# Block attention and the residual: transposed blocks that cross on chip instead of through DRAM

## The chip, the core and the metric

The kernel runs on one core of a Trainium2 chip, in one launch. The metric is the device time in microseconds of an execution; a profile of one execution lies beside it. The engines are TensorE (PE), VectorE (DVE), ScalarE (ACT), GpSimd (POOL) and SyncE (SP), which issues most of the DMA.

## The reference

A chain of four mixers over 256 tokens of width 1024, in fp32: gated linear attention, then a SwiGLU and a gate, differential attention, again a SwiGLU and a gate, a short convolution, and block attention. What is changed lies in the last one and in the residual between all of them:

```python
def moba_mixer(h, w_in, q_gain, k_gain, w_out):      # 16 heads of 64; 256 tokens are one block
    q, k, v, z = jnp.split(h @ w_in, 4, axis=-1)
    q = rms_norm_2(heads(q), q_gain) * (HEAD_DIM ** -0.5)
    k = rms_norm_2(heads(k), k_gain)
    ...
        s_own = jnp.einsum('hqd,hkd->hqk', qc, k_own)
        s_own = jnp.where(own_dist[None] >= 0, s_own - slopes * own_dist, NEG)
        p = jax.nn.softmax(scores, axis=-1)
        ... jnp.einsum('hqk,hkd->hqd', p_own, v_own)
    y = out * jax.nn.silu(z)
    return y @ w_out
# around every mixer and feed-forward part: h = h + f(rms_norm(h, g))
```

The product of probabilities and values needs the probabilities with the keys on the partitions, and each projection needs h with its columns on the partitions: both are transposes.

## The kernel before, in words

**Weights.** All weights are one stream of 512 KB units. SP fetches unit n into one of 4 buffers of `raw` (`fetch`, L438), once VectorE has split the unit that lay there. ScalarE rounds a unit to `whi` (L671), VectorE takes the rest as `wlo` (L1079), in 8 buffers each, and TensorE runs 12 matmuls of 512 columns per unit (L1801): high with high, low with high, high with low. A unit of the block attention's stage is called by its number u from the stage's start (`END[MB_IN]`); there are 40.

**Order.** Each engine runs its program in order. In the block attention the order of the rest is a list by hand, `MB_ORDER`: an entry (u, step, arg) is run by TensorE ahead of unit u; ScalarE first rounds the units below u + 7 and VectorE first splits those below u + 6 (`AHEAD` is 6). SP runs in order too: what it waits for holds up every fetch behind it.

**Probabilities.** For two heads at a time TensorE makes the scores, VectorE adds the distance term and takes the maximum (`max`, L1661 to L1669), ScalarE the exponential (`exp`, L1022) into `mp` (4 buffers). Heads 8 to 15 are turned by TensorE (`pT`). Heads 0 to 7 (`MB_DIRECT`) are turned otherwise: VectorE turns 32x32 blocks in one instruction (`blk`, L1677) into `mblk` (2 buffers, a view of `p_tok`), and then the blocks have to change partitions. GpSimd's queue writes `mblk` to DRAM (`mb_out`, L627) and reads it back, block row by block row, into `mpT` (4 buffers, `mb_in`, L634). TensorE multiplies it with the values (`av`, two heads each, L2253), once `mb_land` says that both heads have landed. GpSimd's program holds the order of these trips and of the norms' powers (`mb_powers`, L599).

**Residual.** The second half of h (`second_blocks`, six times) and the first half behind the first part of a gate (`gate_blocks`, twice) go the same way on SP's queue: VectorE turns blocks into `hblk` (L1119, L1404), SP writes two parts to DRAM (L499, L512), waits for each, reads them back into `hland` (L502, L515), and ScalarE and VectorE make the high and low parts from it (L704 and L1133; L876 and L1414).

Of the kernel before, what the change touches and what calls it, by code (L numbers as in the profile page):

```python
# [17 lines left out]
F32 = mybir.dt.float32  # L18
# [5 lines left out]
P = 128  # L24
SEQ, D = 256, 1024
TT = SEQ // P
KT = D // P
NW = 512
# [6 lines left out]
B = 32  # L35
# [33 lines left out]
UNITS = END[-1]  # L69
# [15 lines left out]
def plan(first, tiles, steps, ends_first=False):  # L85
# [91 lines left out]
        (3, "sums", 0), (8, "sums", 1), (8, "unit", 0), (8, "unit", 1), (12, "max", 0), (12, "max", 1),  # L177
        (13, "blk", 0), (13, "max", 2), (14, "blk", 1), (15, "blk", 2), (16, "sums", 2), (17, "max", 3),
        (17, "max", 4), (17, "max", 5), (17, "blk", 3), (17, "blk", 4), (18, "unit", 2), (18, "max", 6),
        (18, "max", 7), (19, "sums", 3), (20, "blk", 5), (21, "blk", 6), (22, "unit", 3), (25, "max", 8),  # L180
        (25, "blk", 7), (25, "max", 9), (27, "max", 10), (27, "max", 11), (29, "zn", 0), (29, "zn", 1),
        (29, "max", 12), (30, "max", 13), (31, "y", 0), (31, "y", 1), (31, "max", 14), (31, "max", 15),
        (31, "ylo", 0), (32, "zn", 2), (32, "zn", 3), (33, "ylo", 1), (33, "y", 2), (33, "ylo", 2), (34, "y", 3),
        (35, "ylo", 3),),
}


# [53 lines left out]
def build(nc, stream, x, p, cols_d, rows_d, consts_d, wgate_d, out):  # L241
    ctx = ExitStack()
    with ctx:
# [37 lines left out]
        s = phase()  # L281
# [115 lines left out]
        h_dram = nc.dram_tensor("h_blocks", (4, P, 2 * NW), F32, kind="Internal").ap()  # L397
        cv_dram = nc.dram_tensor("cv_blocks", (8, P, NW), F32, kind="Internal").ap()
        mb_dram = nc.dram_tensor("mb_blocks", (MB_DIRECT, P, 3 * P), F32, kind="Internal").ap()
        s_dram = nc.dram_tensor("second_blocks", (len(PAIRED), 2, P, NW), F32, kind="Internal").ap()  # L400
        g_dram = nc.dram_tensor("gate_blocks", (2, TT, P, NW), F32, kind="Internal").ap()
        ffn_dram = nc.dram_tensor("ffn_blocks", (2 * FT, P, NW), F32, kind="Internal").ap()

        block = ctx.enter_context(nc.Block())
# [7 lines left out]
        def _(sp):  # L412
# [67 lines left out]
            def half_blocks(n, tile):  # L480
# [8 lines left out]
                             .rearrange("(i p w) -> p i w", i=P // B, p=P)).then_inc(sem("h_land"), 16)  # L489
                return at + 2  # L490

            def second_blocks(r, tile):

                at = END[tile] + (7 if tile == CV_IN else 8)
                fetch(done, at)
                s = PAIRED.index(tile)
                for q in range(2):
                    sp.wait_ge(sem("g_blk"), 2 * r + q + 1)
                    sp.dma_start(s_dram[s, q], sblk[:, q, :]).then_inc(sem(f"g_out{q}"), 16)  # L499
                for q in range(2):  # L500
                    sp.wait_ge(sem(f"g_out{q}"), 16 * (r + 1))
                    sp.dma_start(sland[:, q, :, :], s_dram[s, q].rearrange("q n -> (q n)")  # L502
                                 .rearrange("(i p w) -> p i w", i=P // B, p=P)).then_inc(sem(f"g_land{q}"), 16)
                return at

            def gate_blocks(n, tile):

                at = END[tile + 2] + 8
                fetch(done, at)
                for t in range(TT):  # L510
                    sp.wait_ge(sem("g_blk"), 2 * (2 * n + 1) + t + 1)
                    sp.dma_start(g_dram[n, t], gblk[:, t, :]).then_inc(sem(f"g_out{t}"), 16)  # L512
                for t in range(TT):
                    sp.wait_ge(sem(f"g_out{t}"), 16 * (2 * n + 2))
                    sp.dma_start(gland[:, t, :, :], g_dram[n, t].rearrange("q n -> (q n)")  # L515
                                 .rearrange("(i p w) -> p i w", i=P // B, p=P)).then_inc(sem(f"g_land{t}"), 16)
                return max(done, at)

            c = Count(sem)
# [29 lines left out]
            upto(done, END[MB_IN])  # L549
            done = max(done, END[MB_IN])  # L550
            done = second_blocks(5, MB_IN)
            fetch(done, UNITS)
            for t in range(TT):
                sp.wait_ge(sem("h_new"), 28 + t + 1)
# [8 lines left out]
        @block.gpsimd  # L563
        def _(pool):
            c = Count(sem)

            def step(ins):
                ins.then_inc(sem("pool_step"), 1)
                c.wait(pool, "pool_step", c.up("pool_step"))

            def power(src, mean, dst, n, scale, eps=EPS):

                step(nc.gpsimd.tensor_scalar(mean, src, scale, eps, ALU.mult, ALU.add))
                return nc.gpsimd.tensor_tensor(dst, mean, neg_half[:, 0:n], ALU.pow)

            def row_norm(j):

                pool.wait_ge(sem("stats"), 4 * (j + 1))
                step(nc.gpsimd.tensor_tensor(ms[:, j, 0, :], stats[:, j, 0, :], stats[:, j, 1, :], ALU.add))  # L579
                power(ms[:, j, 0, :], ms[:, j, 1, :], rstd[:, j, :], TT, 1.0 / D).then_inc(sem("rstd"), 1)  # L580

            step(nc.gpsimd.memset(ident, 0.0))
            nc.gpsimd.affine_select(ident, ident, pattern=[[-1, P]], compare_op=ALU.not_equal, fill=1.0, base=0,
                                    channel_multiplier=1).then_inc(sem("ident"), 1)
            nc.gpsimd.memset(neg_half[:, :], -0.5).then_inc(sem("pool_step"), 1)
            c.wait(pool, "pool_step", c.up("pool_step"))
            row_norm(0)
            for hd in range(GLA_H):
                pool.wait_ge(sem("gla_sq"), TT * (hd + 1))
                both = slice(hd, TT * GLA_H, GLA_H)  # L590
                power(oss[:, 0, both], oss[:, 1, both], oss[:, 2, both], TT, 1.0 / GLA_HV)\
                    .then_inc(sem("gla_rstd"), 1)
            for j in (1, 2, 3):
                row_norm(j)

            def head_power(m, k, ss, dst, sig_ss, signal):

                pool.wait_ge(sem(sig_ss), TT * m + k + 1)
                nc.gpsimd.tensor_tensor(dst, ss[:, 0, k * 8:(k + 1) * 8], neg_half[:, 0:8], ALU.pow)\  # L599
                    .then_inc(sem(signal), 1)  # L600

            def df_onorm(n):

                pool.wait_ge(sem("df_oss"), n + 1)
                nc.gpsimd.tensor_tensor(dss[:, 2, 4 * n:4 * n + 4], dss[:, 1, 4 * n:4 * n + 4], neg_half[:, 0:4], ALU.pow)\
                    .then_inc(sem("df_orstd"), 1)

            for _, what, arg in df_order("pool"):
                if what == "sums":
                    for k in range(TT):  # L610
                        at = slice(k * 8, (k + 1) * 8)
                        dst = dqr[:, arg // 3, at] if arg in (0, 3) else dss[:, 2, at]
                        head_power(arg, k, dss, dst, "df_ss", "df_rstd")
                elif what == "osums":
                    df_onorm(arg)
            for j in (4, 5, 6, 7):
                row_norm(j)

            def mb_powers(t):

                for k in range(TT):
                    head_power(t, k, mss, mss[:, 1 + t % 2, k * 8:(k + 1) * 8], "mb_ss", "mb_rstd")

            def mb_out(hd):

                pool.wait_ge(sem("mb_blk"), hd + 1)
                nc.gpsimd.dma_start(mb_dram[hd], mblk[:, hd % 2, :]).then_inc(sem(f"mb_out{hd % 2}"), 16)  # L627

            def mb_in(hd):

                pool.wait_ge(sem(f"mb_out{hd % 2}"), 16 * (hd // 2 + 1))
                if hd >= 4:
                    pool.wait_ge(sem("mb_av"), hd // 2 - 1)
                nc.gpsimd.dma_start(mpT[:, hd % 4, :].rearrange("p (i w) -> p i w", i=P // B),  # L634
                                    mb_dram[hd].rearrange("q n -> (q n)").rearrange("(i p w) -> p i w", i=P // B, p=P))\
                    .then_inc(sem(f"mb_land{hd // 2 % 2}"), 16)

            mb_powers(0)
            mb_powers(1)
            mb_out(0)  # L640
            mb_out(1)
            mb_in(0)
            mb_out(2)
            mb_in(1)
            mb_powers(2)
            mb_out(3)
            mb_in(2)
            mb_out(4)
            mb_in(3)
            mb_powers(3)  # L650
            mb_out(5)
            mb_out(6)
            for hd in (4, 5, 6):
                mb_in(hd)
            mb_out(7)
            mb_in(7)


        @block.scalar
        def _(act):  # L660
# [36 lines left out]
            def second_hi(j, dst, r, base):  # L697

                split_to(base + 8)
                for q in range(2):  # L700
                    act.wait_ge(sem(f"g_land{q}"), 16 * (r + 1))
                    for k in range(2):
                        kt = 4 + 2 * q + k
                        A(dst[0][:, kt, :].rearrange("p (t i b) -> p t i b", t=TT, b=B),  # L704
# [108 lines left out]
            def ffn(n, src):  # L813
# [46 lines left out]
                for half in range(2):  # L860
# [8 lines left out]
                    if half == 0:  # L869
# [1 line left out]
                        split_to(END[t + 2] + 2 + AHEAD)  # L871
                        squares(j + 1, 0)
                        for k in range(TT):
                            act.wait_ge(sem(f"g_land{k}"), 16 * (2 * n + 2))
                            for kt in range(4):
                                last = A((Y if src is X else X)[0][:, kt, k * P:(k + 1) * P].rearrange("p (i b) -> p i b", b=B),  # L876
                                         gland[:, k, :, kt * B:(kt + 1) * B], ACT.Copy, scale=norm_gain(j + 1)(kt))
# [192 lines left out]
        def _(dve):  # L1070
# [601 lines left out]
            def mb_blocks(hd):  # L1672

                dve.wait_ge(sem("mb_exp"), TT * (hd + 1))
                if hd >= 2:
                    dve.wait_ge(sem(f"mb_out{hd % 2}"), 16 * (hd // 2))
                V.transpose(mblk[:, hd % 2, :].rearrange("p (f n b) -> p f n b", f=P // B, b=B),  # L1677
                            mp[:, hd % 4, :].rearrange("p (n b f) -> p f n b", n=3, b=B)).then_inc(sem("mb_blk"), 1)
# [63 lines left out]
        def _(pe):  # L1742
# [495 lines left out]
            def mb_av(i):  # L2238
# [1 line left out]
                if i % 4 == 0:  # L2240
                    pe.wait_ge(sem("mb_in"), TT * (3 + 3 * (i // 4)))
                if 2 * i < MB_DIRECT:
                    pe.wait_ge(sem(f"mb_land{i % 2}"), 2 * 16 * (i // 2 + 1))
                else:
                    pe.wait_ge(sem("mb_pT"), 2 * (i + 1) - MB_DIRECT)
                if i % 2 == 0:
# [136 lines left out]
```

## Time and profile before

| | |
|---|---|
| median of 3 runs | 901.46 us (901.18 to 901.63) |
| the profiled execution, its span | 900.89 us, 898.7 us |
| busy: DVE, ACT, POOL | 654.6, 506.1, 63.4 us |
| DMA: bytes, mean rate | 187.47 MB, 209 GB/s |
| DRAM trips: `mb_blocks` | 8 out and 8 back, 192 KB each, GpSimd's queue |
| DRAM trips: second and gate blocks | 12 out and 12 back, 256 KB each, SP's queue |
| TensorE's granted clock | full speed (2.4 GHz) in all slices |

Times of a row are microseconds from the span's start unless it says ns. A row of a timeline merges like instructions that follow one another (x is their count), and gives in brackets how long the engine was idle before them and what ended that. The modelled ends of matmuls overlap the next ones.

### The profile page before, as it was taken

To read this page: it belongs to the slowest core of one execution; us is meant where nothing else is said; L and a number is where in the kernel's file an instruction comes from. 1 tells how busy PE (TensorE), PEld (TensorE's weight loads), DVE (VectorE), ACT (ScalarE), POOL (GpSimd) and SP (SyncE) were. 2 spreads that over 40 slices of the span, in tenths; PEclk is the share of its full clock that TensorE was granted. 3 is DMA by queue.
4 is the path that set the end of the run, shared out by engine and by line. 5 is a ranking of instruction groups with operands and counts; after the bars stand their busy time and mean duration, and the time that the engine had idled before them with its cause. 6 is when DMAs were issued, how large, how long until landed. Compare 5 with 4: busy or idle time off the path is not lost.

```text
span 898.7 us, 12238 instructions
## 1 busy us (share of the span) xinstructions
PE 892.9 (99%) x4364; PEld 737.0 (82%) x4364; DVE 654.6 (73%) x997; ACT 506.1 (56%) x820; POOL 63.4 (7%) x75
## 2 busy tenths in 40 slices
PE   9999999999999999999999999999999999999998
PEld 8988888888888888778888888888888888887777
DVE  6985478777735699997787776646679897779764
ACT  6756555444444667688564444435664544587681
POOL 0001000000000003211100000000010000215100
PEclk9999999999999999999999999999999999999999
DMA  7674458766755655424487667746568775656621
GB/s 271 197 240 143 162 189 301 277 242 243 240 194 194 227 199 201 160 97 141 139 284 265 237 239 246 254 142 231 202 220 278 260 253 192 207 200 234 227 70 47
DMA packets 76988, 187.47 MB, mean 209 GB/s; under 512 B 6852, under 2 KB 31812, under 8 KB 76936
## 3 DMA queue, kind: packets, MB, share of 16 engines
q1 hardware_dynamic: 75480, 182.99, 59.6%
q0 software_dynamic: 1024, 3.15, 1.0%
q10 hardware_dynamic: 432, 0.66, 0.2%
q8 instruction: 31, 0.51, 0.2%
q14 instruction: 21, 0.17, 0.1%
HBM read 171.83 MB, written 14.94 MB: 208 GB/s over the span
## 4 chain that ended last, share of the span: by engine, by line
PE 95%; DMA 2%; issue 2%; DVE 1%; POOL 1%; ACT 0%; DVEq 0%; POOLq 0%
PE bank L1801 84%; PE bank L1839 3%; PE bank L1854 1%; PE bank L2114 1%; PE bank L2140 1%; DMA mb_pT<-mb_blocks 1%; DMA mb_blocks<-p_tok 1%; DMA h<-x_dram 0%; PE bank L2224 0%; PE bank L2125 0%; PE bank L2253 0%; PE bank L1961 0%; PE bank L2009 0%; PE bank L2013 0%; PE bank L2100 0%
## 5 line engine op out<-in xcount | busy, mean ns | idle before, releaser
L671 ACT ACTIVATE whi<-raw 128x1024 fp32r<-128x1024 f32 x295 | 306.2, 1060 | 186.3 <-DMA raw<-stream_dram 108.8
L1079 DVE TENSOR_TENSOR wlo<-raw,whi 128x1024 fp32r<-128x1024 f32 x295 | 347.5, 1213 | 55.6 <-ACT whi L671 54.8
L1801 PE MATMUL bank<-whi,x_hi 128*128 128x512 f32 x560 | 152.5, 394 | 0.0
L1801 PE MATMUL bank<-wlo,x_hi 128*128 128x512 f32 x560 | 149.9, 389 | 0.0
L1801 PE MATMUL bank<-whi,x_lo 128*128 128x512 f32 x560 | 149.8, 389 | 0.0
L1801 PEld LDWEIGHTS bank<-wlo,x_hi 128*128 128x128 f32 x560 | 105.1, 188 | 22.3
L1801 PEld LDWEIGHTS bank<-whi,x_lo 128*128 128x128 f32 x560 | 105.1, 188 | 22.0
L1801 PEld LDWEIGHTS bank<-whi,x_hi 128*128 128x128 f32 x560 | 103.4, 188 | 21.7 <-issue 1.2
L1801 PE MATMUL bank<-whi,y_hi 128*128 128x512 f32 x396 | 108.0, 394 | 0.1
L1801 PE MATMUL bank<-wlo,y_hi 128*128 128x512 f32 x396 | 106.0, 390 | 0.0
L1801 PE MATMUL bank<-whi,y_lo 128*128 128x512 f32 x396 | 106.0, 389 | 0.0
L1801 PEld LDWEIGHTS bank<-wlo,y_hi 128*128 128x128 f32 x396 | 74.3, 188 | 15.7
L1801 PEld LDWEIGHTS bank<-whi,y_lo 128*128 128x128 f32 x396 | 74.3, 188 | 15.7
L1801 PEld LDWEIGHTS bank<-whi,y_hi 128*128 128x128 f32 x396 | 72.8, 188 | 16.0 <-issue 0.8
L824 ACT ACTIVATE ffn_silu<-bank,rstd 128x256 f32<-128x256 f32 x44 | 18.4, 471 | 76.8 <-PE bank L1801 76.8
L1303 DVE SCALAR_TENSOR_TENSOR ffn_mid<-bank,rstd,ffn_silu 128x256 f32<-128x256 f32 x44 | 19.3, 479 | 54.0 <-ACT ffn_silu L824 54.0
L1801 PE MATMUL bank<-whi,mid_hi 128*128 128x512 f32 x176 | 47.0, 389 | 0.0
L1801 PE MATMUL bank<-wlo,mid_hi 128*128 128x512 f32 x176 | 47.0, 389 | 0.0
L1801 PE MATMUL bank<-whi,mid_lo 128*128 128x512 f32 x176 | 47.0, 389 | 0.0
L1109 DVE TENSOR_TENSOR h<-h,bank 128x512 f32<-128x512 f32 x22 | 14.1, 683 | 44.7 <-PE bank L1801 44.5
L579 POOL TENSOR_TENSOR ms<-stats 128x2 f32<-128x2 f32 x8 | 4.9, 611 | 577.1 <-ACT junk L718 577.1
L1801 PEld LDWEIGHTS bank<-wlo,mid_hi 128*128 128x128 f32 x176 | 33.0, 188 | 6.9
(251 smaller groups left out, 891.4 us busy)
## 6 DMA issues: line engine op xcount, KB each, us to landing
raw<-stream_dram SPq DMA_DIRECT2D x295, 512.0 KB, 4.6
ffn_blocks<-ffn_blk SPq DMA_DIRECT2D x22, 256.0 KB, 2.0
ffn_land<-ffn_blocks SPq DMA_DIRECT2D x22, 256.0 KB, 3.7
second_blocks<-h_blk SPq DMA_DIRECT2D x8, 256.0 KB, 2.0
h_land<-second_blocks SPq DMA_DIRECT2D x8, 256.0 KB, 3.1
cv_blocks<-cv_blk SPq DMA_DIRECT2D x7, 256.0 KB, 5.2
cv_land<-cv_blocks SPq DMA_DIRECT2D x7, 256.0 KB, 3.3
h_blocks<-h_blk SPq DMA_DIRECT2D x3, 512.0 KB, 6.3
```

Of the source, the lines that this page charges most:

```text
L579: step(nc.gpsimd.tensor_tensor(ms[:, j, 0, :], stats[:, j, 0, :], stats[:, j, 1, :], ALU.add))
L671: A(whi[:, u % RING, :], raw[:, u % RAW, :], ACT.Copy).then_inc(sem("w_hi"), 1)
L824: A(sg[:, (t - tin) % 2, k, :], bank[2 * (t % 2) + k][:, 0:256], ACT.Silu, scale=rstd[:, j, k:k + 1]).then_inc(sem("ffn_silu"), 1)
L1079: V.tensor_tensor(wlo[:, u % RING, :], raw[:, u % RAW, :], whi[:, u % RING, :].bitcast(F32), ALU.subtract).then_inc(sem("w_lo"), 1)
L1109: V.tensor_tensor(h[:, t, half * HALF:(half + 1) * HALF], h[:, t, half * HALF:(half + 1) * HALF], bank[2 * (tile % 2) + t][:, :], ALU.add) ...
L1303: V.scalar_tensor_tensor(mid[:, (t - tin) % 2, :, k, :], bank[2 * (t % 2) + k][:, 256:512].rearrange("p (k n) -> p k n", k=2), rstd[:, j, ...
L1801: last = T.matmul(bank[pair + t][:, :], lhs[a][:, kt, t * P:(t + 1) * P], w[:, u % RING, kk * NW:(kk + 1) * NW], start=part != 1 and k == ...
L1839: last = T.matmul(bank[pair + hd // 2][:, hd % 2 * SEQ:(hd % 2 + 1) * SEQ], w[:, u % RING, kk * NW + hd * P:kk * NW + (hd + 1) * P], lhs[a ...
L1854: last = T.transpose(bank[b][:, k * SEQ + t * P:k * SEQ + (t + 1) * P], src[:, t, kt * P:(kt + 1) * P], ident)
L2114: last = T.matmul(bank[DF_S_BANKS[hd][m]][:, q * SEQ:(q + 1) * SEQ], dT[r, 0, hd, q * P:(q + 1) * P], dT[r, 1, hd, :], start=True, stop=True)
L2140: last = T.matmul(bank[b][:, q * SEQ + (hd % 2) * P:q * SEQ + (hd % 2 + 1) * P], daT[:, hd % 4, k * SEQ + q * P:k * SEQ + (q + 1) * P], dv ...
```

## The change

Heads 4 to 7 no longer go through DRAM. SP issues four transfers for each, one for every 32 partitions of `mblk`, straight into `mpT`; they stand at u = 22, 23, 26 and 27 of a new list for SP, behind the fetch of the units below u + 10, and wait for the block and for the `av` that frees the buffer of `mpT`. GpSimd's trips for these heads go. VectorE's `blk` of heads 5, 6 and 7 move from u = 20, 21 and 25 to 18, 24 and 24; those of 6 and 7 wait until heads 4 and 5 have crossed (`mblk` has two buffers). The residual's trips of the two kinds become four direct transfers per part (`cross`), without the wait between. Heads 0 to 3, the feed-forward's and the convolution's trips and `half_blocks` stay.

```diff
-        (18, "max", 7), (19, "sums", 3), (20, "blk", 5), (21, "blk", 6), (22, "unit", 3), (25, "max", 8),
-        (25, "blk", 7), (25, "max", 9), (27, "max", 10), (27, "max", 11), (29, "zn", 0), (29, "zn", 1),
+        (18, "max", 7), (18, "blk", 5), (19, "sums", 3), (22, "unit", 3), (24, "blk", 6), (24, "blk", 7),
+        (25, "max", 8), (25, "max", 9), (27, "max", 10), (27, "max", 11), (29, "zn", 0), (29, "zn", 1),
...
+    "sp": (
+        (22, "cross", 4), (23, "cross", 5), (26, "cross", 6), (27, "cross", 7),),
...
+            def cross(dst, src, signal):
+
+                for i in range(P // B):
+                    sp.dma_start(dst[:, i, :], src[i * B:(i + 1) * B, :]).then_inc(sem(signal), 16)
...
                 for q in range(2):
                     sp.wait_ge(sem("g_blk"), 2 * r + q + 1)
-                    sp.dma_start(s_dram[s, q], sblk[:, q, :]).then_inc(sem(f"g_out{q}"), 16)
-                for q in range(2):
-                    sp.wait_ge(sem(f"g_out{q}"), 16 * (r + 1))
-                    sp.dma_start(sland[:, q, :, :], s_dram[s, q].rearrange("q n -> (q n)")
-                                 .rearrange("(i p w) -> p i w", i=P // B, p=P)).then_inc(sem(f"g_land{q}"), 16)
+                    cross(sland[:, q, :, :], sblk[:, q, :], f"g_land{q}")
...
             done = second_blocks(5, MB_IN)
+            for u, _, hd in mb_order("sp"):
+                fetch(done, min(u + 10, UNITS))
+                done = max(done, min(u + 10, UNITS))
+                sp.wait_ge(sem("mb_blk"), hd + 1)
+                sp.wait_ge(sem("mb_av"), hd // 2 - 1)
+                for i in range(P // B):
+                    sp.dma_start(mpT[:, hd % 4, i * 3 * B:(i + 1) * 3 * B], mblk[i * B:(i + 1) * B, hd % 2, :])\
+                        .then_inc(sem(f"mb_cross{hd % 2}"), 16)
             fetch(done, UNITS)
...
-            mb_out(4)
             mb_in(3)
             mb_powers(3)
-            mb_out(5)
-            mb_out(6)
-            for hd in (4, 5, 6):
-                mb_in(hd)
-            mb_out(7)
-            mb_in(7)
...
                 dve.wait_ge(sem("mb_exp"), TT * (hd + 1))
-                if hd >= 2:
+                if hd >= 6:
+                    dve.wait_ge(sem(f"mb_cross{hd % 2}"), 64)
+                elif hd >= 2:
                     dve.wait_ge(sem(f"mb_out{hd % 2}"), 16 * (hd // 2))
...
-                    pe.wait_ge(sem(f"mb_land{i % 2}"), 2 * 16 * (i // 2 + 1))
+                    if i < 2:
+                        pe.wait_ge(sem(f"mb_land{i % 2}"), 2 * 16)
+                    else:
+                        pe.wait_ge(sem("mb_cross0"), 64 * (i - 1))
+                        pe.wait_ge(sem("mb_cross1"), 64 * (i - 1))
```

The gate's trips change as the second half's; ScalarE's waits for both count 64 where they counted 16.

## Rows read from the trace of the kernel before

**Rows 1.** The page, busy us of each engine, its share and instructions

```profile
PE 892.9 (99%) x4364; PEld 737.0 (82%) x4364; DVE 654.6 (73%) x997; ACT 506.1 (56%) x820; POOL 63.4 (7%) x75
```

**Rows 2.** TensorE's longest waits over the run: us in total, times, longest

```profile
PE bank L1897 <- DVE gla_r L1149: 1.2, 1, 1.2
PE bank L2253 <- DMA mb_pT<-mb_blocks: 1.1, 2, 0.7
PE bank L2100 <- issue: 0.3, 1, 0.3
```

**Rows 3.** Timeline of TensorE, 838 to 853: start, length, what

```profile
838.63 1.07 PE L1801 MATMUL bank<-whi,x_lo 128*128 128x512 f32 x4
840.35 0.87 PE L2253 MATMUL bank<-mb_pT,mb_v 128*64 128x256 f32 x8 [0.66 <-DMA mb_pT<-mb_blocks]
...
850.78 1.08 PE L1801 MATMUL bank<-whi,x_lo 128*128 128x512 f32 x4
852.27 0.87 PE L2253 MATMUL bank<-mb_pT,mb_v 128*64 128x256 f32 x8 [0.41 <-DMA mb_pT<-mb_blocks]
```

**Rows 4.** Timeline of GpSimd, 826 to 848

```profile
826.99 3.27 POOL L599 TENSOR_TENSOR mb_ss<-mb_ss,neg_half 128x8 f32<-128x8 f32 x2 [4.02 <-DVE mb_ss L1460]
...
835.18 0.76 POOL L634 DMA_DIRECT2D mb_pT<-mb_blocks  x1 [2.26 <-DMA mb_blocks<-p_tok]
...
847.04 0.75 POOL L634 DMA_DIRECT2D mb_pT<-mb_blocks  x1 [1.89 <-DMA mb_blocks<-p_tok]
```

**Rows 5.** Landing: mb_pT; raw from 825 to 850; second_blocks out (L499); back (L502)

```profile
DMA to landing us min/median/max: 3.2/5.3/5.9
DMA to landing us min/median/max: 3.2/5.1/5.8
DMA to landing us min/median/max: 2.0/2.0/2.0
DMA to landing us min/median/max: 2.6/3.1/4.3
```

**Rows 6.** Timeline of VectorE, 828 to 848

```profile
828.56 0.87 DVE L1677 STREAM_TRANSPOSE p_tok<-mb_p 128x384 f32<-128x384 f32 x1
829.35 1.18 DVE L1079 TENSOR_TENSOR wlo<-raw,whi 128x1024 fp32r<-128x1024 f32 x1
...
842.11 0.56 DVE L1661 SCALAR_TENSOR_TENSOR mb_s<-consts,bank 128x384 f32<-128x384 f32 x1 [4.14 <-PE bank L2224]
...
843.43 0.87 DVE L1677 STREAM_TRANSPOSE p_tok<-mb_p 128x384 f32<-128x384 f32 x1
...
845.49 2.35 DVE L1079 TENSOR_TENSOR wlo<-raw,whi 128x1024 fp32r<-128x1024 f32 x2
```

**Rows 7.** Timeline of SP: fetches of raw 31, 32 and 35

```profile
832.45 0.33 SPq L438 DMA_DIRECT2D raw<-stream_dram  x1
834.79 0.33 SPq L438 DMA_DIRECT2D raw<-stream_dram  x1
846.73 0.33 SPq L438 DMA_DIRECT2D raw<-stream_dram  x1
```

**Rows 8.** Windows: length, busy of each engine, TensorE's clock, DMA share, GB/s

```profile
830.00:840.00 10.00, 9.70 (x50) 7.65 (x46) 7.12 (x8) 7.60 (x11) 3.63 (x6) 1.00 0.95 330
840.00:855.00 15.00, 14.24 (x85) 10.38 (x86) 10.56 (x22) 8.78 (x20) 1.31 (x2) 1.00 0.51 180
```

**Rows 9.** Last second_blocks, then first gate_blocks: ScalarE and TensorE; SP for the gate

```profile
769.54 0.91 ACT L704 ACTIVATE x_hi<-h_land,cols 128x256 fp32r<-128x256 f32 x2 [3.40 <-DMA h_land<-second_blocks]
773.07 1.07 PE L1801 MATMUL bank<-whi,x_hi 128*128 128x512 f32 x4
...
319.02 0.33 SPq L512 DMA_DIRECT2D gate_blocks<-h_blk  x1
325.08 1.28 ACT L876 ACTIVATE y_hi<-h_land,cols 128x128 fp32r<-128x128 f32 x4 [1.48 <-DMA h_land<-gate_blocks]
327.61 1.16 PE L1801 MATMUL bank<-whi,y_hi 128*128 128x512 f32 x4
```

More of the change, by code:

```diff
@@ L399, in build @@
         mb_dram = nc.dram_tensor("mb_blocks", (MB_DIRECT, P, 3 * P), F32, kind="Internal").ap()
-        s_dram = nc.dram_tensor("second_blocks", (len(PAIRED), 2, P, NW), F32, kind="Internal").ap()
-        g_dram = nc.dram_tensor("gate_blocks", (2, TT, P, NW), F32, kind="Internal").ap()
         ffn_dram = nc.dram_tensor("ffn_blocks", (2 * FT, P, NW), F32, kind="Internal").ap()
@@ L495, in second_blocks @@
                 fetch(done, at)
-                s = PAIRED.index(tile)
                 for q in range(2):
                     sp.wait_ge(sem("g_blk"), 2 * r + q + 1)
-                    sp.dma_start(s_dram[s, q], sblk[:, q, :]).then_inc(sem(f"g_out{q}"), 16)
-                for q in range(2):
-                    sp.wait_ge(sem(f"g_out{q}"), 16 * (r + 1))
-                    sp.dma_start(sland[:, q, :, :], s_dram[s, q].rearrange("q n -> (q n)")
-                                 .rearrange("(i p w) -> p i w", i=P // B, p=P)).then_inc(sem(f"g_land{q}"), 16)
+                    cross(sland[:, q, :, :], sblk[:, q, :], f"g_land{q}")
                 return at
@@ L511, in gate_blocks @@
                     sp.wait_ge(sem("g_blk"), 2 * (2 * n + 1) + t + 1)
[L512 to L516, printed above, removed]
+                    cross(gland[:, t, :, :], gblk[:, t, :], f"g_land{t}")
                 return max(done, at)
@@ L631, in mb_in @@
                 pool.wait_ge(sem(f"mb_out{hd % 2}"), 16 * (hd // 2 + 1))
-                if hd >= 4:
-                    pool.wait_ge(sem("mb_av"), hd // 2 - 1)
                 nc.gpsimd.dma_start(mpT[:, hd % 4, :].rearrange("p (i w) -> p i w", i=P // B),
@@ L700, in second_hi @@
                 for q in range(2):
-                    act.wait_ge(sem(f"g_land{q}"), 16 * (r + 1))
+                    act.wait_ge(sem(f"g_land{q}"), 64 * (r + 1))
                     for k in range(2):
@@ L873, in ffn @@
                         for k in range(TT):
-                            act.wait_ge(sem(f"g_land{k}"), 16 * (2 * n + 2))
+                            act.wait_ge(sem(f"g_land{k}"), 64 * (2 * n + 2))
                             for kt in range(4):
```

## The prediction

> **What bounds the kernel now.** I read the page's busy times first: TensorE is busy for 892.9 of the span's 898.7 us [rows 1]. A change to transfers adds and removes no matmul, so it can only act on the 5.8 us in which TensorE is idle. The waits of TensorE over the whole run say what these are [rows 2]: the only ones that transfers of the changed kind end are two at L2253, 1.1 us together, for mb_pT. The reader is to see that no residual trip is in that list. The timeline of TensorE places the two [rows 3]: av(2) starts at 840.35 after 0.66 us idle and av(3) at 852.27 after 0.41 us. The modelled end of the matmuls before them hides about 0.1 us of each (back to back, the next group starts 0.91 us after the last: 838.63 + 0.91 = 839.54 and 850.78 + 0.91 = 851.69, so at most 0.81 and 0.58). **The most that this change can give by these waits is therefore 1.1 to 1.4 us, 0.12 to 0.15%.** A measurement of this kernel tells about 0.2%, 1.8 us, from no change; the forecast can hardly leave that band on the fast side.
>
> Next come the views of what ends the two waits. GpSimd's timeline [rows 4]: head 5's way back from DRAM is issued at 835.18, head 7's at 847.04. 835.18 + 5.2 is the end of the first wait, 847.04 + 5.2 that of the second (the trips back land in 3.2 to 5.9, median 5.3 [rows 5]). VectorE's timeline [rows 6] says why head 7 is so late: it stands idle for 4.14 us until TensorE's scores(4), turns max(8), and only at 843.43 turns blk(7), though the list has the exponentials of head 7 at u = 20.
>
> **The change part by part** (times are those of the profiled execution: 900.89 us with a span of 898.7; the median of the runs shown is 901.46, 0.57 above it, and I add that at the end).
>
> *Heads 4 to 6 in VectorE's order.* One transpose takes a place of 0.79 us (828.56 to 829.35 [rows 6]). blk(5) now stands ahead of the split of unit 24, so this split, that of unit 25 and sums(3) are 0.79 late; after blk(5)'s old place all is on time again, and after blk(6)'s old place 0.79 early. Late splits send raw 28 and 29 0.79 late, both before 830 still, while TensorE takes unit 28 only behind av(3), after 852 [rows 3]: hidden under 20 us. GpSimd's powers, which wait for sums(3), end at 831.05 instead of 830.26 [rows 4]. VectorE's unit(3), which waits for them, stood two splits of 1.1 and blk(6) behind 829.35, at 832.34, and now at 831.55: hidden with 0.5 to spare, and late by what is over that if the cover is gone.
>
> *Cross 4 and 5 on SP.* SP has to have fetched raw 31 before cross 4 and raw 32 before cross 5. These were issued at 832.45 and 834.79, each behind a split [rows 7]; 0.79 earlier that is 831.66 and 834.00. The waits added are met by then: the blocks of heads 4 and 5 are turned at u = 17 and 18 of VectorE's list, ahead of these splits, and av(0) stands at u = 22, three units ahead of the av(2) that TensorE reaches at 839.54. (At three units of 2.72 us, three groups of 0.907, it is about 8 us earlier, 831; if it came later, cross 4 and all behind it would wait with it.) An issue takes 0.33 us on SP [rows 7], four take 1.3: cross 4 until 833.3, ahead of raw 32; cross 5 from 834.3 to 835.65; raw 33, queued behind it, can go at 835.65; its split, about 1.15 behind that of raw 32 (two take 2.35 [rows 6]), allows it at 835.15: held 0.5, less than the 0.79 that its split is early. So no weight is late by SP.
>
> *How long a direct transfer takes* is not in this trace: none goes from SBUF to SBUF. From the last issue to the landing I bound it by 2.0 us below (a 256 KB write of h_blk, always 2.0 [rows 5]) and 5.8 above (raw in this stretch, 3.2 to 5.8 [rows 5]); I exclude less than 2.0, since the transfer still has a read and a write side like that one. Value taken: 3.1, the median of the read that puts 512-byte pieces on 128 partitions [rows 5], the nearest in form. The load matters: the DMA engines are 95% busy from 830 to 840 at 330 GB/s, 51% from 840 to 855 [rows 8]. The change takes one of the two trips of each head away, 192 KB or 0.6 us at that rate, so the crowd thins a little. Head 5 thus lands at 835.65 + 3.1 = 838.75 (837.65 to 841.45). TensorE is there at 839.54: the first wait goes; at the upper end it is 1.9 instead of 0.8.
>
> *The added waits on VectorE.* blk(6) now waits for cross 4 and blk(7) for cross 5, and behind them on VectorE stand the split of unit 30 and max(8). The cover is the 4.14 us in which VectorE waited for scores(4) anyway. blk(7) and that split take 0.79 + 1.14, so max(8) can start at 838.75 + 2.0 = 840.75; scores(4) releases it at 842.11 - 0.8 = 841.3 if TensorE is earlier. So max(8) at M = 841.3, and the wait costs nothing until head 5 lands later than 839.3. With 5.8 us M is 843.45.
>
> *Cross 6 and 7.* In the old order the split of unit 31 starts at 845.49, 3.38 after max(8); with blk(7) no longer between them 2.59. Raw 35 followed the start of that split by 1.24 [rows 6, 7]: now M + 3.83 = 845.1. Then SP issues cross 6 (1.3), raw 36 at 846.8 (0.5 later than its split allows, for a unit that TensorE takes eight units behind av(3)), cross 7 at 847.1 to 848.45. Landing with 3.1: 851.55 (850.45 to, with both late, 843.45 + 7.15 + 5.8 = 856.4). TensorE, 0.81 earlier, reaches av(3) at 850.9. Of the second wait 0.65 us stays instead of 0.58.
>
> *Sum at av(3):* it starts at 851.6 instead of 852.27: 0.7 us gained; with 2.0 us transfers everything, up to 1.4; with 5.8 us ones 4.1 lost. What is late next is the same wait, at the same place, for a transfer on another queue.
>
> *The residual's trips* (six second_blocks, two gate_blocks). Each replaces four issues of 0.33 us [rows 9] and a wait for writes that land in 2.0 [rows 5] by eight issues: 2.6 us of SP against 1.3 and the part of 2.0 that the second issue doesn't cover. Raw is at most some 0.5 later by that, a fifth of a unit's 2.72. At the last of the six ScalarE waited 3.40 us for the first part, had it at 769.54 and was done at 770.45; TensorE takes it at 773.07 [rows 9], 2.6 us later. From the trip before (2.0 + 0.33 + 2.6 to 4.3, 4.9 to 6.6) to the direct one (1.3 + 2.0 to 5.8, 3.3 to 7.1) the landing moves by -3.3 to +2.2: TensorE gets nothing and loses nothing. The tightest of the eight is the first gate trip: ScalarE has its last part from 325.08, is done with it at 326.36, and TensorE takes it at 327.61 [rows 9]. Direct, issued at 319.02 to 320.3, it lands at 322.3 to 326.1, at worst 1.0 after today, inside 1.25. I cost all eight at nothing.
>
> *A rule against it.* The trace's raw loads 31 and 32 are issued 2.34 us apart, and raw lands in 3.2 to 5.8 there [rows 5, 7], so neighbours on SP's queue overlap. The Trainium skill, "DMA: Bandwidth & Descriptors", "Rules for kernel authors", says that transfers under 64 KB mostly pay overhead and that two transfers to disjoint halves of the partitions serialize, so that one is to be used; each piece here is 48 KB. If the overhead overlaps as for raw, the sum above holds; if it is paid four times in a row, rival 3 does.
>
> **Rivals.**
> 1. *The wait is only moved.* Cross 7 stands on SP behind raw 35 and 36, two 512 KB loads, where GpSimd's queue passed them. If it lands 4 us after its last issue, at 852.45, av(3) starts where it did: 901.5. For it: median 5.1 of raw here [rows 5]; against: DMA only half busy after 840 [rows 8]. Taken with all outcomes from 0.2 gained to 1.8 lost.
> 2. *Slower by one chain through VectorE.* blk(7) holds VectorE until head 5 has landed; beyond 839.3 each us delays max(8), the splits 31 and 32, raw 35 and 36, and with them cross 7, which then also lands late. It decides when a transfer takes over about 4.7 us from its last issue: head 5 at 840.35, M = 842.35, av(3) at 842.35 + 7.15 + 4.7 = 854.2, 1.9 lost. With 5.5: 841.15, 843.15, 855.8, 3.5 lost: 905.0. For it: 95% load before 840 [rows 8]; against: 3.1 for the similar read.
> 3. *The four don't overlap.* 4 x 2.0 from the first issue: head 5 at 842.3, M = 844.3, cross 7 issued from 850.1 and landed at 858.1: 5.8 lost, 907.3. Against it: the overlap of the raws.
> 4. *More than 1.8 us faster* needs TensorE idle time that its waits don't list; I see none.
>
> **How the numbers follow.** Forecast, 0.2 to 1.4 gained, 0.58; rival 1, 0.27; rival 2, 0.09; rival 3, 0.03; rival 4, 0.03. Time: 901.46 - 0.7 = 900.8 (a profile of 900.2). Range: from 901.46 - 1.4 = 900.0 to 901.46 + 1.3 = 902.8, which leaves out the last two rivals and the worse part of rival 2. Faster by over 0.2%: 0.03; slower: 0.09 + 0.03 = 0.12; the rest, 0.85, within 0.2%.
>
> **What would show it.** In the profile after: L2253's wait at av(2) gone and one of at most 0.8 us left at av(3), on a direct transfer; VectorE waiting at blk(6) or blk(7) up to about 839.5 and no longer as much at max(8); raw 35 issued near 845 instead of 846.73; direct landings of 3 to 4 us from the first of the four; ScalarE's waits at L704 some 2 us shorter each and TensorE unmoved by them. Landings over 5 us, a wait of several us at av(2) or av(3), or a TensorE wait at a residual trip would make it wrong.

## The result

| | this kernel | the kernel before |
|---|---|---|
| median of 13 runs each | 904.41 us (902.96 to 905.58) | 901.18 us (899.37 to 904.40) |
| ratio, 95% interval | 1.0037 (1.0028 to 1.0045) | |
| the profiled execution, its span | 904.99 us, 903.0 us | 900.89 us, 898.7 us |

The change made the kernel 3.2 us slower. The forecast was 900.8, and 902.8 was its upper end: it was wrong, on the side of rival 2.

The page's busy times, against [rows 1]:

```profile
PE 894.8 (99%) x4364; PEld 739.1 (82%) x4364; DVE 655.0 (73%) x997; ACT 507.6 (56%) x820; POOL 59.6 (7%) x67
```

The span grew by 4.3 us and TensorE's busy time by 1.9 with the same 4364 matmuls: some is new waiting, some the same matmuls at a lower clock. TensorE's longest waits (us in total, times, longest; L2254 is the old L2253):

```profile
PE bank L2254 <- DMA mb_pT<-p_tok: 2.2, 1, 2.2
PE bank L1894 <- DVE gla_r L1144: 1.2, 1, 1.2
PE bank L2254 <- issue: 1.1, 1, 1.1
```

Two waits stand at the place of [rows 2], and both are longer. The profile names a direct transfer for one of them only; the other, at av(2), ends at 841.29, the moment at which VectorE's blk(7) starts behind the crossing of head 5 (841.30, below). TensorE's timeline (start, length, what; idle before it in brackets), against [rows 3]:

```profile
841.29 0.87 PE L2254 MATMUL bank<-mb_pT,mb_v 128*64 128x256 f32 x8 [1.05 <-issue]
...
855.04 0.87 PE L2254 MATMUL bank<-mb_pT,mb_v 128*64 128x256 f32 x8 [2.24 <-DMA mb_pT<-p_tok]
...
861.42 1.08 PE L1798 MATMUL bank<-whi,x_hi 128*128 128x512 f32 x4
```

This execution runs 0.54 us late from before the crossings (the scores that started at 814.95 start at 815.49); that differs from execution to execution, and an execution of the change with other residual shapes (`shapes`, below) has 815.02. av(2) is 0.94 later than before, 0.40 beyond that; av(3) 2.77 later, 1.83 more; the unit that started at 857.08 is 4.34 later, another 1.57. The windows (length, busy us of PE, PEld, DVE, ACT and POOL with counts, TensorE's granted clock, DMA share, GB/s) show what the last step is:

```profile
855.00:857.00 2.00, 1.96 (x17) 1.31 (x18) 0.97 (x3) 0.89 (x2) 0.00 (x0) 0.89 0.83 322
857.00:859.00 2.00, 2.00 (x7) 1.71 (x7) 1.77 (x5) 1.27 (x2) 0.00 (x0) 0.50 0.44 180
859.00:861.00 2.00, 2.00 (x8) 1.56 (x8) 1.23 (x1) 1.97 (x4) 0.00 (x0) 0.76 0.00 0
861.00:863.00 2.00, 2.00 (x10) 1.64 (x9) 0.91 (x3) 1.90 (x5) 0.00 (x0) 1.00 0.78 250
```

The clock falls to half, 1.2 GHz, behind the idle time at av(3), for some 3.4 us in all (2.00 x (0.11 + 0.50 + 0.24), over 0.5); before, it was 1.00 here. So the 4.3 us are 0.54 + 0.40 + 1.83 + 1.57.

Why head 7 came late is read from SP's timeline, against [rows 7]:

```profile
832.66 2.51 SPq L554 DMA_DIRECT2D mb_pT<-p_tok  x4
835.22 0.59 SPq L438 DMA_DIRECT2D raw<-stream_dram  x1
835.90 3.13 SPq L554 DMA_DIRECT2D mb_pT<-p_tok  x4
...
847.07 0.33 SPq L438 DMA_DIRECT2D raw<-stream_dram  x1
847.50 2.49 SPq L554 DMA_DIRECT2D mb_pT<-p_tok  x4
850.03 0.59 SPq L438 DMA_DIRECT2D raw<-stream_dram  x1
851.04 2.49 SPq L554 DMA_DIRECT2D mb_pT<-p_tok  x4
```

Four direct issues hold SP for 2.5 to 3.1 us, not 1.3, and a fetch right behind them 0.59 instead of 0.33. The groups by line (ns of one issue, min/median/max, first and last start; then the landing in us, counted from the start of the issue): the probabilities, then the residual.

```profile
L554 SPq DMA_DIRECT2D mb_pT<-p_tok x16: 542/603/1247, 832.7 to 852.9; - x16
DMA to landing us min/median/max: 2.0/2.8/4.7
L495 SPq DMA_DIRECT2D h_land<-h_blk x48: 542/603/662, 123.0 to 769.6; - x48
DMA to landing us min/median/max: 2.1/2.1/2.6
```

On the way itself the direct transfers are not slow: 2.0 to 4.7, where the way back from DRAM alone took 3.2 to 5.9 [rows 5].

VectorE's timeline, against [rows 6], shows the delay being passed on:

```profile
839.35 0.88 DVE L1674 STREAM_TRANSPOSE p_tok<-mb_p 128x384 f32<-128x384 f32 x1 [3.59 <-DMA mb_pT<-p_tok]
841.30 0.89 DVE L1674 STREAM_TRANSPOSE p_tok<-mb_p 128x384 f32<-128x384 f32 x1 [1.07 <-DMA mb_pT<-p_tok]
...
843.21 0.55 DVE L1656 SCALAR_TENSOR_TENSOR mb_s<-consts,bank 128x384 f32<-128x384 f32 x1
...
845.83 2.35 DVE L1074 TENSOR_TENSOR wlo<-raw,whi 128x1024 fp32r<-128x1024 f32 x2
```

The first two are blk(6), waiting for head 4's crossing, and blk(7), for head 5's. max(8) and the split of unit 31 stand behind them, raw 35 waits for that split, cross 6 stands behind raw 35 and cross 7 behind raw 36. **So the late end of the first two crossings comes back, through VectorE and SP's fetches, as a late start of the last two**, which then pay the same price again.

### The profile page after: what moved, and what is told of

Its sections match the earlier page's. It is cut to its first block, busy times and chain, and to the rows that moved or that the text cites. A ratio compares the mean times of both kernels' runs of the same rounds, so it can differ in the third digit from the quotient of the medians.

```text
span 903.0 us, 12271 instructions
## 1 busy us (share of the span) xinstructions
PE 894.8 (99%) x4364; PEld 739.1 (82%) x4364; DVE 655.0 (73%) x997; ACT 507.6 (56%) x820; POOL 59.6 (7%) x67
## 3 DMA queue, kind: packets, MB, share of 16 engines
q0 software_dynamic: 512, 1.57, 0.5%
## 4 chain that ended last, share of the span: by engine, by line
PE 94%; DVE 3%; DMA 1%; issue 1%; SPq 1%; ACT 0%; ACTq 0%; DVEq 0%
PE bank L1798 82%; PE bank L1836 3%; PE bank L1851 1%; DVE wlo L1074 1%; PE bank L2111 1%; PE bank L2137 1%; SPq L554 1%; DMA mb_pT<-p_tok 1%; DMA raw<-stream_dram 1%; PE bank L2221 0%; PE bank L2122 0%; PE bank L2254 0%; PE bank L1894 0%; DVE mb_tok L1462 0%; PE bank L1958 0%
## 5 line engine op out<-in xcount | busy, mean ns | idle before, releaser
L583 POOL TENSOR_TENSOR ms<-stats 128x2 f32<-128x2 f32 x8 | 1.8, 228 | 580.0 <-ACT junk L713 580.0
```

## The experiments

Theory A: an issue on SP between two places in SBUF costs 0.60 us instead of 0.33, and the order couples the last crossings to the first. Rivals: the residual's transfers do it; direct transfers are slow on the way; the shape of a piece sets the price; any queue would do as badly. Ratios are to the kernel before on the same chip; its medians there were 901.55 (23 runs; `residual_only`, `block_only`, `uncoupled`, `shapes`), 901.46 (35 runs; `pairs`, `pairs_behind`, `on_gpsimd`, `dram_earlier`) and 900.64 (15 runs; `dram_quarters`, `pairs_sums_first`). They are not the quotients of the two medians and differ from these by up to 0.001.

**One part alone: the residual.** (`residual_only`) Block attention as before.

```diff
-                    sp.dma_start(s_dram[s, q], sblk[:, q, :]).then_inc(sem(f"g_out{q}"), 16)
-                ... (the wait and the way back)
+                    cross(sland[:, q, :, :], sblk[:, q, :], f"g_land{q}")
```

> Only the residual's trips direct; heads 4 to 7 go through DRAM on GpSimd's queue as before. Theory A: no change within 0.1% (-0.5 to +0.7 us): SP is held some 5 us per trip, but TensorE has no wait there. Rival B: +1 us or more, with a new wait of TensorE or weights late near 130, 325, 450, 650, 660 or 770 us.

901.72 us (12 runs), 0.9995 (0.9984 to 1.0006): no difference that the interval shows.

**One part alone: block attention.** (`block_only`) The changed kernel with the residual's trips through DRAM.

```diff
-                    cross(sland[:, q, :, :], sblk[:, q, :], f"g_land{q}")
+                    sp.dma_start(s_dram[s, q], sblk[:, q, :]).then_inc(sem(f"g_out{q}"), 16)
+                ... (the wait and the way back)
```

> Only the block attention's part of the change (SP list, four direct transfers for each of heads 4 to 7, the blocks turned sooner); the residual's trips go through DRAM as before. Theory A (the block attention's crossings on SP cost all of it: each of their issues holds SP about 0.6 us instead of the 0.33 that I took, so cross 7 lands some 2 us late, and TensorE's clock falls behind the long wait): as much slower than before as the whole change, +2.5 to +4 us, with a wait of about 2 us at av(3). Rival B (the residual's 48 transfers, which now hold SP 5 us per trip, make weights late somewhere): clearly less than the whole change, under +2 us.

904.63 us (5 runs), 1.0036 (1.0023 to 1.0049): the whole loss. Its timeline of TensorE has the same late av(3):

```profile
855.27 0.87 PE L2260 MATMUL bank<-mb_pT,mb_v 128*64 128x256 f32 x8 [2.19 <-DMA mb_pT<-p_tok]
```

**The coupling cut.** (`uncoupled`) The last crossings stand ahead of raw 35 and 36; price and number of the issues stay.

```diff
-        (22, "cross", 4), (23, "cross", 5), (26, "cross", 6), (27, "cross", 7),),
+        (22, "cross", 4), (23, "cross", 5), (24, "cross", 6), (24, "cross", 7),),
```

> The whole change, but cross 6 and 7 stand at u = 24 in SP's list (behind raw 33 instead of raw 35 and 36): the same transfers at the same price on SP. Theory A with its second half (the place behind raw 35 and 36, whose splits follow max(8) and max(9), is what makes head 7 late): cross 7 is issued from about 843 and lands by 848, av(3) does not wait, TensorE's clock stays at full speed, only the wait of about 1 us at av(2) is left: before -0.5 to +0.8 us. Rival C (the price on SP alone, wherever the transfers stand: SP is held 10 us in this stage and weights or VectorE are late by it): still +1.5 us or more.

901.33 us (11 runs), 0.9995 (0.9986 to 1.0004): the loss is gone. TensorE's timeline, then SP's:

```profile
841.90 0.87 PE L2254 MATMUL bank<-mb_pT,mb_v 128*64 128x256 f32 x8 [0.95 <-issue]
...
853.38 0.87 PE L2254 MATMUL bank<-mb_pT,mb_v 128*64 128x256 f32 x8
```

```profile
837.32 2.48 SPq L554 DMA_DIRECT2D mb_pT<-p_tok  x4
839.85 0.59 SPq L438 DMA_DIRECT2D raw<-stream_dram  x1
840.54 6.24 SPq L554 DMA_DIRECT2D mb_pT<-p_tok  x8
```

The eight last issues span 6.24 us, but are done at 846.8 instead of 853.5. av(3) waits for nothing; av(2) still does (it starts with VectorE's blk(7), at 841.90, behind the crossing of head 5).

**Half the issues.** (`pairs`) Two heads cross in one set of four pieces of 96 KB; for that the blocks of two heads lie interleaved in `mblk` and `mpT`.

```diff
-        (22, "cross", 4), (23, "cross", 5), (26, "cross", 6), (27, "cross", 7),),
+        (22, "cross", 4), (24, "cross", 6),),
...
-                    sp.dma_start(mpT[:, hd % 4, i * 3 * B:(i + 1) * 3 * B], mblk[i * B:(i + 1) * B, hd % 2, :])\
+                    sp.dma_start(mpT2[:, hd // 2 % 2, i * 6 * B:(i + 1) * 6 * B], mblk2[i * B:(i + 1) * B, :])\
```

> Two heads per transfer as in pairs_behind, and the second set at u = 24, behind raw 33. Theory A: neither wait is left, av(2) and av(3) start without idle time: before -0.8 to -1.6 us (about 900.3 for a before of 901.5). Rival D: a wait at av(2) stays because the larger transfers land later: before +-0.5 us.

900.28 us (12 runs), 0.9986 (0.9977 to 0.9994). Its list of TensorE's longest waits has no transfer; an issue of twice the bytes costs the same:

```profile
PE bank L1897 <- DVE gla_r L1147: 1.2, 1, 1.2
PE bank L2210 <- DVE mb_tok L1465: 0.5, 1, 0.5
```

```profile
L557 SPq DMA_DIRECT2D mb_pT<-p_tok x8: 549/603/631, 833.5 to 843.1; - x8
```

**Half the issues, coupling kept.** (`pairs_behind`) As pairs, with the last crossing behind the fetches again.

```diff
-        (22, "cross", 4), (24, "cross", 6),),
+        (22, "cross", 4), (27, "cross", 6),),
```

> The change with two heads per transfer: the blocks of heads 4 and 5 (6 and 7) lie side by side, so four transfers of 96 KB carry both; they stand at u = 22 and at u = 27, behind raw 36 as the change's cross 7. SP's time for heads 4 to 7 is halved (8 issues in place of 16), the place of the last behind raw 35 and 36 is kept. Theory A (the price of an issue on SP, times sixteen, in the chain through VectorE and SP): head 5 lands about 838, max(8) is at about 842, the last transfers are issued from 847.5 to 850 and land at about 852: a wait of at most 0.8 us at av(3), clock at full speed, before -0.8 to +0.5 us. Rival D (the place behind raw 35 and 36 alone costs it, whatever the price; or a transfer twice as large holds SP twice as long): still +1.5 us or more.

902.15 us (12 runs), 1.0009 (0.9998 to 1.0020). Its interval lies under the changed kernel's (1.0028 to 1.0045), but reaches from the kernel before to rival D's 1.5 us, so the wait decides. av(3) waits half as long as in the changed kernel, though longer than theory A's 0.8:

```profile
852.96 0.87 PE L2256 MATMUL bank<-mb_pT,mb_v 128*64 128x256 f32 x8 [1.07 <-DMA mb_pT<-p_tok]
```

So the two causes act together, and each can be taken away by itself: cutting the coupling removes the wait at av(3) and leaves the one at av(2); halving the issues removes the one at av(2) and halves the one at av(3); only both together (`pairs`) leave none.

**Another queue.** (`on_gpsimd`) The same 16 transfers, issued by GpSimd behind its powers.

```diff
+            for hd in range(4, MB_DIRECT):
+                pool.wait_ge(sem("mb_blk"), hd + 1)
+                pool.wait_ge(sem("mb_av"), hd // 2 - 1)
+                ... nc.gpsimd.dma_start for the four pieces; SP's list is empty
```

> The change with the same 16 direct transfers issued by GpSimd instead of SP, each behind the same waits; SP only fetches. Theory A (SP's time is what they cost): both waits gone or under 0.3 us, before -0.5 to -1.6 us. Rival E (a direct transfer is slow by itself, on any queue, or GpSimd issues four as slowly: 0.55 to 0.75 us each): a wait of 0.5 us or more at av(2) stays: before -0.5 to +0.5 us or worse.

904.57 us (12 runs), 1.0025 (1.0014 to 1.0036): slow again, against theory A, at the other wait. GpSimd's timeline, then TensorE's:

```profile
828.44 6.03 POOL L595 TENSOR_TENSOR mb_ss<-mb_ss,neg_half 128x8 f32<-128x8 f32 x2 [4.77 <-DVE mb_ss L1453]
834.43 4.39 POOL L648 DMA_DIRECT2D mb_pT<-p_tok  x8
```

```profile
843.52 1.55 PE L2252 MATMUL bank<-mb_pT,mb_v 128*64 128x256 f32 x8 [3.12 <-DMA mb_pT<-p_tok]
```

An issue costs 0.55 us here (4.39 over 8). On this queue that is no price of the kind: in the kernel before, its writes of 192 KB to DRAM cost as much.

```profile
L627 POOL DMA_DIRECT2D mb_blocks<-p_tok x8: 540/554/758, 806.3 to 844.6; - x8
```

The powers ahead of the issues took 6.03 us instead of 3.27 [rows 4], which I had not reckoned with, so the first issue comes 1.8 us later than SP's (834.43 against 832.66). Even so the eight are out by 838.82, no later than SP's (839.03). What is late is the landing of head 5: av(2) starts 4.7 us after the last issue is done, against 2.3 in the changed kernel. Here the time on the way makes most of the wait; why it is longer is open. The run therefore doesn't say what SP's time alone is worth.

**What shape costs.** (`shapes`) One execution, 904.69 us: the residual's pieces in other shapes (the output is then another permutation of the blocks).

```diff
+                    elif form == "straight":
+                        sp.dma_start(dst[:, i, :], src[:, i * P:(i + 1) * P]).then_inc(sem(signal), 16)
+                    ... (32 partitions to the same 32; 64 partitions to 128)
```

> The whole change, but the residual's direct transfers have other shapes (the first second half: 128 partitions of 512 bytes to the same partitions; the first gate as in the change, 32 partitions of 2 KB to 128 of 512 bytes; the second second half: 32 partitions of 2 KB to the same 32; the second gate: 64 partitions of 1 KB to 128 of 512 bytes; the last two second halves as in the change), so the data that these put into h's transposed form is another permutation and the output is not the reference's. If the price of 0.54 to 0.66 us per issue comes from one source row being cut over four partitions, the straight and the quarter form take about 0.33 and the half form something between; if it comes from a transfer within SBUF as such, all take 0.54 to 0.66.

In turn: 128 partitions to the same 128, 32 to the same 32, 64 to 128, and 32 to 128 as in the change:

```profile
L498 SPq DMA_DIRECT2D h_land<-h_blk x8: 560/601/610, 122.4 to 126.9; - x8
L500 SPq DMA_DIRECT2D h_land<-h_blk x8: 590/591/607, 447.1 to 451.5; - x8
L503 SPq DMA_DIRECT2D h_land<-h_blk x8: 523/603/617, 641.8 to 646.6; - x8
L496 SPq DMA_DIRECT2D h_land<-h_blk x24: 553/603/1410, 317.2 to 769.3; - x24
```

None of the four shapes sets the price.

**The same pieces with DRAM at one end.** (`dram_quarters`) The kernel before, whose residual goes out and back in four pieces of 64 KB each.

```diff
-                    sp.dma_start(s_dram[s, q], sblk[:, q, :]).then_inc(sem(f"g_out{q}"), 16)
+                    for i in range(P // B):
+                        sp.dma_start(s_dram[s, q][i * B:(i + 1) * B, :], sblk[i * B:(i + 1) * B, q, :])\
+                            .then_inc(sem(f"g_out{q}"), 16)
... (the way back and both ways of the gate's trips in four pieces too)
```

> The kernel before, whose residual trips still go through DRAM, but each part goes out in four pieces of 64 KB and comes back in four pieces of 64 KB, so that SP issues pieces as small and as narrow (32 partitions on the side of the blocks) as the direct ones. Theory A, the 0.60 us belong to a transfer with both ends in SBUF: an issue takes 0.27 to 0.37 us, as the kernel before shows for other transfers with DRAM at one end. Rival, the price goes with small or narrow pieces, whatever their ends: 0.54 to 0.66 us for the pieces out, the pieces back, or both. The time says little: the second issue out to the last one back lengthens the trip by about 1.3 us by theory A, inside the 2.6 us that TensorE had; 901.5, and up to 903 by the rival.

One execution. Pieces out, then back:

```profile
L500 SPq DMA_DIRECT2D second_blocks<-h_blk x32: 324/426/926, 122.4 to 773.5; - x32
L505 SPq DMA_DIRECT2D h_land<-second_blocks x32: 319/432/516, 126.0 to 777.5; - x32
```

0.43 us lies between the two theories, and neither held whole. What adds 0.1 is not the size but the place in the row: the first piece of a trip, with nothing right ahead of it, took 0.33 (first line), as a whole 256 KB part did in the kernel before (second line), and there too four 512 KB fetches right behind one another took 0.43 or more (third line).

```profile
122.38 0.33 SPq L500 DMA_DIRECT2D second_blocks<-h_blk  x1
L499 SPq DMA_DIRECT2D second_blocks<-h_blk x8: 326/326/327, 122.6 to 765.8; - x8
L438 SPq DMA_DIRECT2D raw<-stream_dram x4: 430/467/884, 126.0 to 127.5; - x4
```

So both ends in SBUF cost 0.17 more in a row (0.60 against 0.43), and 0.2 more for one that stands by itself (0.54 at 851.04 in the changed kernel, against 0.33). The time missed the expectation by far: 906.35 us. TensorE's waits say where:

```profile
PE bank L1809 <- ACT ple_gate L875: 3.4, 2, 2.2
```

At the first gate trip ScalarE has its last part at 327.29, 2.2 later than 325.08 [rows 9], and TensorE waited all of these 2.2 us. So there was no slack of 1.25 us: ScalarE's `ple_gate`, which TensorE also waits for, stands right behind that part, and in the kernel before it ended at 327.50, just ahead of 327.61. ScalarE before, then TensorE in this run:

```profile
326.26 1.24 ACT L867 ACTIVATE ple_gate<-bank,rstd 128x512 f32<-128x512 f32 x2
329.81 1.17 PE L1809 MATMUL bank<-whi,y_hi 128*128 128x512 f32 x4 [2.21 <-ACT ple_gate L875]
```

The direct trip stays clear of this because its last part comes earlier, not later: 324.80 in the changed kernel.

**Without direct transfers: only head 7 earlier.** (`dram_earlier`) The kernel before with one entry moved.

```diff
-        (25, "blk", 7),
+        (24, "blk", 7),   # ahead of (25, "max", 8)
```

> The kernel before, all through DRAM, with only head 7's block turned ahead of max(8) (u = 24). By the order alone head 7 goes out at about 838, is back by 846, and the wait of 0.41 us at av(3) goes, the one of 0.66 at av(2) stays: before -0.3 to -0.7 us, which the interval may not tell from zero. If this does as much as the direct transfers in their best place, what is to be had lies in the order and not in the way on chip.

901.48 us (12 runs), 1.0002 (0.9990 to 1.0015). The wait at av(3) goes, but the one at av(2) grows from 0.66 to 1.26:

```profile
842.68 0.87 PE L2253 MATMUL bank<-mb_pT,mb_v 128*64 128x256 f32 x8 [1.26 <-DMA mb_pT<-mb_blocks]
...
854.12 0.87 PE L2253 MATMUL bank<-mb_pT,mb_v 128*64 128x256 f32 x8
```

The way back of head 5 landed in 6.3 us here (issued at 836.35), not in 5.2. So the order alone did not bring what `pairs` brought.

**Pairs, with the powers' input earlier.** (`pairs_sums_first`) In pairs VectorE's unit(3) waited 1.53 us for the powers, and TensorE 0.5 at L2210 behind it.

```diff
-        (18, "blk", 5), (19, "sums", 3), (22, "unit", 3),
+        (19, "sums", 3), (19, "blk", 5), (22, "unit", 3),
```

> The pairs version with sums(3) ahead of the transpose of head 5 again in VectorE's list, as before the change: GpSimd's powers can start 0.8 us earlier. In the pairs version TensorE waited 0.5 us at L2210 for work of VectorE that had waited 1.5 us for the powers. If the order of sums(3) made this wait: it goes, or falls by 0.5, and the time is 899.8 (899.4 to 900.3). If the powers' own length makes it (two took 6.0 us in that kernel against 3.3 in the kernel before): the wait stays at 0.2 to 0.5 and the time at 900.3. The two are 0.5 us apart, so the profile's wait decides and not the time. Against the kernel before both give about 0.9985.

900.14 us (11 runs), 0.9993 (0.9984 to 1.0002). The wait at L2210 has left the list. GpSimd's row shows two differences at once: the powers start 1.05 us earlier than in pairs (829.15; 0.33 of that is the two executions' offset) and take 3.91 us instead of 6.02. What of the wait went by the earlier start and what by the length stays open.

```profile
828.10 3.91 POOL L606 TENSOR_TENSOR mb_ss<-mb_ss,neg_half 128x8 f32<-128x8 f32 x2 [3.77 <-DVE mb_ss L1458]
```

Pairs is the one version whose interval lies wholly under the kernel before, by 0.14%. pairs_sums_first, which has none of these waits either, is not told from it: the gain is at the edge of what was measured.

## Why the prediction was wrong

The step that failed is the term "an issue takes 0.33 us on SP, four take 1.3". It was read from fetches of `raw` out of DRAM [rows 7] and given to a kind of transfer that the trace does not contain. The landing, of the same unknown kind, was bounded from both sides; the issue was not. Measured: 0.603 (0.542 to 1.247), sixteen times, and 0.59 for a fetch right behind. Part of it could have been read before: the fetches of [rows 7] each came 1.5 us or more behind the one before, while the trace also had four in a row, at 0.43 or more. With that, four would have been 1.6 (0.33 and three times 0.43); the rest, to 2.5, belongs to the new kind. Put into the prediction's own sum (its times are shifted by the 0.54 us of this execution):

| step | forecast | measured |
|---|---|---|
| cross 4 starts | 832.5 | 832.66 |
| cross 5 issued until | 836.2 | 839.03 |
| M, max(8) | 841.8 | 843.21 |
| raw 35 | 845.6 | 847.07 |
| cross 7 issued until | 849.0 | 853.53 |
| av(3) | 852.1 | 855.04 |

Behind cross 4 (2.51 instead of 1.3) raw 32 goes 0.7 late, it takes 0.26 more, and cross 5 takes 1.8 more: 2.8 us. A landing 0.8 shorter than the sum's 3.1 (839.03 to 841.30) and the reserve of 0.55 at VectorE take half of that away, and 1.4 reaches M; the longer issues of cross 6, raw 36 and cross 7 add 2.6, and 0.4 lies between the last two. At the end the landing is 1.5 (853.53 to 855.04), which gives 1.6 back: av(3) is 2.9 late.

Point by point:

- *The most to be gained, 1.1 to 1.4 us:* it fits. Pairs, which takes both waits away, gained 1.2 (0.5 to 2.1).
- *Landing, 3.1 us after the last issue:* too long where it counted, at heads 5 and 7 (2.3 and 1.5), and too short at head 4 (835.17 to 839.35, 4.2), which held nothing up. The lower bound of 2.0 was no bound: the profile counts a landing from the start of its issue, and the sum set it behind the end. The short landings could not make up for the issues.
- *Rival 2, the chain through VectorE:* this is what happened, link by link. Its deciding point was wrong: I let it decide on a landing over 4.7 us, for 0.09. It decided with landings of 2.0 to 4.7 counted from the start of the issue, since the issues before them took twice as long. The sum had put the reserve at VectorE at 0.55 us (839.3 against 838.75); cross 5 was out 2.8 later than forecast, and head 5 landed 2.0 later.
- *Rival 3 and the Trainium skill's rule* ("DMA: Bandwidth & Descriptors", "Rules for kernel authors", small transfers mostly pay overhead): as written, four landings of 2.0 in a row, rival 3 did not happen: the four overlap on their way. But something is paid four times, and I had looked for it in the landing only: what follows one another is their issue, 2.5 us in this trace for 192 KB. The answer that the rule gives, to coalesce, is what pairs did, four transfers of 96 KB for eight of 48.
- *The residual at nothing:* right (0.9995), with a wrong price and in part by luck. A trip holds SP for 5.1 us, not 2.6, and ScalarE's waits are not 2 us shorter each, as the prediction's signs have it: six of them are 12.8 us together before and after. The cover of 1.25 us at the first gate did not exist (`dram_quarters`); it was not needed. At the last trip ScalarE's first part comes at 769.16 (769.54 before [rows 9]) and its second at 771.75 (771.37 before):

```profile
765.15 5.07 SPq L495 DMA_DIRECT2D h_land<-h_blk  x8
769.16 0.91 ACT L699 ACTIVATE x_hi<-h_land,cols 128x256 fp32r<-128x256 f32 x2 [2.65 <-DMA h_land<-h_blk]
```

- *A count was wrong,* ahead of the prediction and in it: second_blocks stands four times, not six, as the x8 of the row of L499 above shows (two parts each); with the two gate trips that is 48 direct transfers. Nothing in the sum used it.
- *GpSimd's powers, "hidden with 0.5 to spare":* not reliable. Two powers took 3.27 us before [rows 4], 4.28 in the changed kernel and 6.0 in five others; in pairs the cover was gone and TensorE paid 0.5. It is the second power that grows. Before, then in pairs:

```profile
828.62 1.64 POOL L599 TENSOR_TENSOR mb_ss<-mb_ss,neg_half 128x8 f32<-128x8 f32 x1
830.79 4.38 POOL L606 TENSOR_TENSOR mb_ss<-mb_ss,neg_half 128x8 f32<-128x8 f32 x1
```

The second takes 1.64 in the four kernels whose VectorE turns a block beside it, 2.64 or 4.4 in the seven whose VectorE, with blk(5) moved ahead, splits three units in a row there, and 2.27 in pairs_sums_first. That the splits hold it up is inferred from this, not tested.
- *Missing altogether:* the clock. The forecast had a wait cost its own length and TensorE's busy time unchanged; it rose by 1.9 us.

## What to carry to other kernels

A transfer has two prices: the time until it lands (here 2.0 to 4.7 us) and the time that its issue holds the queue (here 0.60), and where a kind of transfer is new to a trace, both are unknown and both need bounds. A price read from issues that stand alone need not hold for issues in a row. Several small transfers in place of one multiply the second price, and everything that stands behind them on the queue pays. Before a wait is put ahead of other work, follow what that work releases: here it released, two queues on, the very transfers whose time was in question.

## What the hardware showed

- On SP an issue in a row with both ends in SBUF took 0.60 us, at 48, 64 and 96 KB and in four shapes, against 0.43 with DRAM at one end, for 64 KB pieces and for 512 KB fetches; by itself it took 0.54 against 0.33. A fetch right behind a transfer within SBUF took 0.59. On GpSimd's queue 0.55 was paid for 48 KB within SBUF and for 192 KB to DRAM alike. Why is open.
- After the 2.2 us wait at av(3) the granted clock of the profiled execution fell to half. Of the other runs only the mean clock is known; it is under 1 (0.996 or 0.998) in 8 of 13 runs of the changed kernel (median 905.03, against 903.72 of the other five: 1.3 us), 4 of 5 of block_only and 8 of 12 of on_gpsimd (3.1 us wait). With waits up to 1.3 us it is rare: none of 12 residual_only, 11 uncoupled, 12 pairs and 11 pairs_sums_first, 1 of 12 pairs_behind, 2 of 12 dram_earlier, and 2 of 73 of the kernel before in these batches. That the wait is the cause is inferred from these counts; no run changed the wait alone. The profiled execution of block_only has the wait of 2.19, the one of dram_quarters one of 2.2 at the first gate, and both kept the full clock.
- The same two powers on GpSimd took 3.3 to 6.0 us in different kernels, longest where VectorE split units in a row beside them; no run changed that alone.
